# Down projection with seven block products in place of eight in 13 of 44 groups

## The chip, the core and the metric

The kernel runs on one core of a Trainium2 chip, as one launch. The metric is the device time of a launch in microseconds. TensorE (PE) multiplies, VectorE (DVE), ScalarE (ACT) and GpSimd (POOL) work elementwise, and SyncE (SP) issues nearly all DMAs. All matrices are float32. A product of two of them is made of three matmuls in the fp32r format: each operand is split into a high part (a rounding copy) and a low part (operand minus high part), and high x high, high x low and low x high are added up in PSUM.

## The reference

Three layers over 256 tokens of width 2048. The change touches the last step of the third, the feed-forward network, and the final norm behind it:

```python
h = rmsnorm_2(x, ffn_norm[l])
g = causal_dwconv(jnp.einsum('bsd,df->bsf', h, w_gate[l]), conv_w[l], conv_b[l])
u = jnp.einsum('bsd,df->bsf', h, w_up[l])
x = x + jnp.einsum('bsf,fd->bsd', jax.nn.silu(g) * u, w_down[l])   # f = 5632, d = 2048
return rmsnorm_2(x, final_norm)
```

## The kernel before

All weights stream through the core once, as 691 *units* of mostly 128 x 1024 floats (two K tiles of 128 rows by one block of 512 columns, in the down projection). `plan` lists them in order, and every engine walks the same list. SP loads a unit into one of `NS = 4` staging slots (L3027); ACT writes its high part into one of `NR = 3` slots of `s_w` (L1253), after PE has finished the unit three before; DVE subtracts and writes the low part (L1910); PE multiplies (`down`, L706). A staging slot is free once the low part is made.

On ACT and DVE all other work is *side work*: generators in a list (`Side`), each advanced one step by `side.tick()` before each `split()` in `nxt`. So side work stands in program order ahead of a high or low part. `later(n, steps)` holds a generator back by n steps. Both engines' loops stand three units ahead of PE's: what the code puts after `nxt` for a unit comes behind the low part of the third unit after it.

The feed-forward part runs in two halves: 12 blocks of gate and up (L1862, 8 units each), down projection of 24 K tiles, 10 blocks, down projection of 20 K tiles. A gate or up block leaves PSUM by ACT, is turned by 16 DVE transposes of 32x256 (L2001, four a step), then comes the convolution (L2462, L2464, into `CV` from `GG`), silu on ACT, and the product with up (L2477, into one of two `HH`). ACT copies that to the high part of `HID` (L1672) and POOL makes the low part (L2892). The last up block's side work runs while PE is already in the down projection.

The down projection takes the four 512-column blocks n = 0..3 one after the other; tokens are two halves t of 128. Block n's sums lie in PSUM banks `PSS` (n even) or `PST` (n odd), one bank for each t. When a block is done, DVE adds its two banks into `OT` (L2647), which already holds the residual, brought there in the first half by 64 transposes (`flip`, L2634, two a step). In the second half squares of the finished blocks go to ACT (L1679), and POOL multiplies them by the final gain (L3005). The last block's last three units are ordered so that the tail is short (`last_columns`).

Of the kernel before, what the change touches and what calls it, by code (L numbers as in the profile page):

```python
# [23 lines left out]
NTOT = 691  # L24
WINS = (2, 4, 8, 16)
DOWN = (24, 20)
BLOCKS = (range(12), range(12, 22))
PACE = (2,) * 11 + (1,) * 5
# [152 lines left out]
class Plan:  # L181
# [3 lines left out]
    def __init__(self, A):  # L185
        self.A = A
        self.units, self.end, self.bank, self.out, self.half, self.zb = [], {}, {}, {}, {}, []
        self.takes = 0
        self.turned = {}
        self.counts = {"out": 0, "out_act": 0}  # L190
        self.between = Side()

    def unit(self, ap, n, shift=0):
        self.units.append((ap, n, shift))
# [72 lines left out]
    def down(self, hv):  # L267
        for n in range(4):
            for u in range(DOWN[hv] // 2):
                self.unit(self.A["wd"][2 * DOWN[0] * hv + DOWN[hv] // 2 * n + u], 1024, SHIFT)  # L270
                self.step()
            self.end["wd", hv, n] = len(self.units)
# [90 lines left out]
class Memory:  # L363


    def __init__(self, nc, ctx):
# [122 lines left out]
        self.HID = alloc(ff, "hid", [128, 2, DOWN[0], T], F32R)  # L489
        self.EV = alloc(ff, "ev", [128, 4, 2, 128])  # L490
# [3 lines left out]
        self.HH = [alloc(ff, f"hh{i}", [128, T]) for i in range(2)]  # L494
# [7 lines left out]
        self.FW = alloc(ff, "fw", [128, 2])  # L502
        ff.close()
# [25 lines left out]
    def staged(self, c, n):  # L529
        s = self.ST[:, c % NS, 0:n]  # L530
        return s.rearrange("p (k c) -> p k c", k=KT) if n == KT * 36 else s

# [4 lines left out]
    def product(self, bank):  # L537

        if bank[0] == "g":
            return self.PSG[bank[1]]  # L540
        return (self.PSS if bank[0] == "s" else self.PST)[:, bank[1], :]

# [24 lines left out]
def tensor_program(e, S, P, M):  # L567
# [138 lines left out]
    def down(hv):  # L706
# [36 lines left out]
        for n in range(4):  # L743
            for t in range(2):
                vacant(("st"[n % 2], t))
                held["st"[n % 2], t] = ("added", 2 * (4 * hv + n) + t + 1)
            apart = nk // 2 - (3 if hv and n == 3 else 0)
            for u in range(apart):
                w.wait_ge("wl", done[0] + 1)
                products(n, u, done[0] % NR, [(kk, t) for kk in range(2) for t in range(2)]).then_inc(S["units"], 1)  # L750
                unit()
            c = done[0]
            for u in range(apart, nk // 2):
                w.wait_ge("wl", c + u - apart + 1)
                products(n, u, (c + u - apart) % NR, [(0, 0), (1, 0)])
            if apart < nk // 2:
                last_columns(c)
# [482 lines left out]
def scalar_program(e, S, P, M):  # L1240
    w, side, done = Waits(e, S), Side(), [0]

    def split():

        c = done[0]
        if c >= NTOT:
            return
        done[0] += 1
        _, n, shift = P.units[c]
# [3 lines left out]
        e.activation(M.weights(c, 0, n, shift), M.staged(c, n), ACT.Copy).then_inc(S["wh"], 1)  # L1253
# [79 lines left out]
    def token_norm(n, rc, ticks):  # L1333
# [4 lines left out]
        for t in range(2):  # L1338
            w.wait_ge(f"l_tm{i}", 16)
# [324 lines left out]
    def up_block(m):  # L1664
# [3 lines left out]
        for c in range(4):  # L1668
# [3 lines left out]
            e.activation(M.HID[:, 0, j - DOWN[0] * hv, :], M.HH[j % 2][:, :], ACT.Copy).then_inc(S["hidh"], 1)  # L1672
            yield

    def square_out(n, t):
        w.wait_ge("added", 2 * (4 + n) + t + 1)
        if n:
            w.wait_ge("sqx", 2 * n + t - 1)
        e.activation(M.JK[t][:, :], M.OT[:, t, block(n)], ACT.Square, accum_out=M.SS[:, t, n:n + 1]).then_inc(S["sqx"], 1)  # L1679

# [35 lines left out]
    for half, name in enumerate(("st_a", "st0")):  # L1716
        ws = slice(512 * half, 512 * half + 512)
        e.dma_start(M.ST[:, 0, ws], P.units[0][0][:, ws]).then_inc(S[name], 16)
# [142 lines left out]
    for hv in range(2):  # L1861
# [8 lines left out]
        for n in range(4):  # L1870
            nxt(DOWN[hv] // 2)
            if hv and n == 0:
                tables()
            if hv and n < 3:
                side.start(squares(n))
# [23 lines left out]
def vector_program(e, S, P, M):  # L1899
    w, side, done, chained = Waits(e, S), Side(), [0], [0]  # L1900

    def split():

        c = done[0]
        if c >= NTOT:
            return
        done[0] += 1
        _, n, shift = P.units[c]
# [1311 lines left out]
```

## Time and profile before

| | us |
|---|---|
| median of three runs | 1994.98 (1994.73 to 1996.5) |
| the profiled execution: span | 1993.4 |
| PE busy | 1983.1 (99%) |
| DVE busy | 1544.2 (77%) |
| ACT busy | 1067.4 (54%) |
| POOL busy | 404.5 (20%) |

The profile gives its own execution by the span from first to last instruction, and no device time beside it. Down projections run from 1528.1 to 1658.6 us and from 1876.4 to 1985.6 us. A timeline row has start, duration, engine, line, operation, out<-in, partitions x elements and the count it merges; in brackets stands how long the engine idled before it and what ended that. A matmul's duration (0.39 us) reaches into the next, since they are pipelined: what counts is the distance between starts. "PEld" is the load of the stationary operand.

### The profile page before, as it was taken

What the parts mean: (1) busy time and instruction counts of PE and PEld (TensorE: products, weight loads), DVE (VectorE), ACT (ScalarE), POOL (GpSimd) and SP (SyncE); (2) the same over time, 40 slices, a digit from 0 to 9 for tenths busy, and PEclk for the clock granted to TensorE, in tenths of its full rate; (3) what the DMA queues carried; (4) which work ended last, traced back from release to release, by engine and by line L of the source; (5) the groups of instructions that cost most, each with busy time, mean ns of one, the idle gap of its engine ahead of it and who ended that gap; (6) DMA issues with size and microseconds to landing.
All of it is one profiled execution on the core that took longest, in us unless ns stands there. A gap on an engine that the chain in (4) does not pass through costs nothing.

```text
span 1993.4 us, 26947 instructions
## 1 busy us (share of the span) xinstructions
PE 1983.1 (99%) x10228; PEld 1689.0 (85%) x10228; DVE 1544.2 (77%) x2292; ACT 1067.4 (54%) x1625; POOL 404.5 (20%) x381
## 2 busy tenths in 40 slices
PE   9999999999999999999999999999999999999998
PEld 8888888888888888888788888888888888888887
DVE  6876778788798666867777678689899776889954
ACT  7744544467534554654555555455555434555544
POOL 0015543300000444430222235200000000000121
PEclk9999999999999999999999999999999999999999
DMA  9664666567655334565444445655555655555564
GB/s 359 213 198 150 192 185 198 190 210 244 219 172 170 126 117 134 185 218 185 166 162 155 148 155 188 208 190 197 194 190 190 203 196 185 196 191 191 191 205 153
DMA packets 103506, 374.80 MB, mean 188 GB/s; under 512 B 11696, under 2 KB 13136, under 8 KB 102864
## 3 DMA queue, kind: packets, MB, share of 16 engines
q1 hardware_dynamic: 103088, 372.54, 56.3%
q8 instruction: 81, 1.33, 0.3%
q10 hardware_dynamic: 288, 0.52, 0.1%
q14 instruction: 49, 0.40, 0.1%
HBM read 370.92 MB, written 2.10 MB: 187 GB/s over the span
## 4 chain that ended last, share of the span: by engine, by line
PE 98%; DVE 1%; DMA 0%; ACT 0%; issue 0%; ACTq 0%; SPq 0%
PE psg L601 25%; PE psg L602 13%; PE psg L686 9%; PE psg L688 9%; PE psg L687 9%; PE pss L686 4%; PE pss L688 4%; PE pss L687 4%; PE pss L717 2%; PE pss L716 2%; PE pss L718 2%; PE pst L718 2%; PE pst L716 2%; PE pst L717 2%; PE pst L873 1%; PE psg L662 1%
## 5 line engine op out<-in xcount | busy, mean ns | idle before, releaser
L1253 ACT ACTIVATE s_w<-s_stage 128x1024 fp32r<-128x1024 f32 x689 | 724.0, 1053 | 648.6 <-PE psg L602 288.2
L1910 DVE TENSOR_TENSOR s_w<-s_stage,s_w 128x1024 fp32r<-128x1024 f32 x689 | 855.9, 1244 | 269.0 <-ACT s_w L1253 264.7
L601 PE MATMUL psg<-s_rh,s_w 128*128 128x512 f32 x1216 | 427.4, 393 | 0.3 <-DVE s_w L1910 0.3
L601 PE MATMUL psg<-s_ry,s_w 128*128 128x512 f32 x1024 | 361.6, 394 | 0.0
L602 PE MATMUL psg<-s_rh,s_w 128*128 128x256 f32 x1216 | 342.7, 282 | 0.0
L602 PE MATMUL psg<-s_ry,s_w 128*128 128x256 f32 x1024 | 288.4, 282 | 0.0
L601 PEld LDWEIGHTS psg<-s_rh,s_w 128*128 128x128 f32 x1216 | 228.3, 188 | 48.8 <-issue 1.0
L686 PE MATMUL psg<-s_w,s_ry 128*128 128x512 f32 x672 | 263.9, 393 | 0.0
L688 PE MATMUL psg<-s_w,s_ry 128*128 128x512 f32 x672 | 261.7, 389 | 0.0
L687 PE MATMUL psg<-s_w,s_ry 128*128 128x512 f32 x672 | 261.6, 389 | 0.0
L602 PEld LDWEIGHTS psg<-s_rh,s_w 128*128 128x128 f32 x1216 | 229.8, 189 | 0.7
L601 PEld LDWEIGHTS psg<-s_ry,s_w 128*128 128x128 f32 x1024 | 192.3, 188 | 42.1 <-issue 2.7
L602 PEld LDWEIGHTS psg<-s_ry,s_w 128*128 128x128 f32 x1024 | 193.5, 189 | 0.1
L2892 POOL TENSOR_TENSOR s_hid<-s_hh,s_hid 128x256 fp32r<-128x256 f32 x44 | 49.9, 1134 | 581.7 <-ACT s_hid L1672 581.7
L686 PEld LDWEIGHTS psg<-s_w,s_ry 128*128 128x128 f32 x672 | 126.1, 188 | 27.7 <-issue 1.8
L688 PEld LDWEIGHTS psg<-s_w,s_ry 128*128 128x128 f32 x672 | 126.1, 188 | 26.7
L687 PEld LDWEIGHTS psg<-s_w,s_ry 128*128 128x128 f32 x672 | 126.2, 188 | 25.5
L686 PE MATMUL pss<-s_w,s_ry 128*128 128x512 f32 x352 | 137.1, 390 | 0.0
L688 PE MATMUL pss<-s_w,s_ry 128*128 128x512 f32 x352 | 137.1, 389 | 0.0
L687 PE MATMUL pss<-s_w,s_ry 128*128 128x512 f32 x352 | 137.0, 389 | 0.0
L2760 POOL TENSOR_SCALAR s_bsc<-s_bsc,s_stat 128x256 f32<-128x256 f32 (+1 forms) x56 | 46.0, 839 | 187.4 <-DVE s_stat L2355 176.1
L2001 DVE STREAM_TRANSPOSE s_gg<-s_ev 32x256 f32<-32x256 f32 x176 | 76.7, 436 | 2.9
(445 smaller groups left out, 2897.2 us busy)
## 6 DMA issues: line engine op xcount, KB each, us to landing
s_stage<-in_wo SPq DMA_DIRECT2D x96, 512.0 KB, 3.6
s_stage<-in_wg SPq DMA_DIRECT2D x88, 512.0 KB, 3.2
s_stage<-in_wu SPq DMA_DIRECT2D x88, 512.0 KB, 3.3
s_stage<-in_wd SPq DMA_DIRECT2D x88, 512.0 KB, 3.2
s_stage<-in_ain SPq DMA_DIRECT2D x64, 512.0 KB, 3.6
s_stage<-in_wkv SPq DMA_DIRECT2D x32, 512.0 KB, 4.0
s_stage<-in_bq SPq DMA_DIRECT2D x24, 512.0 KB, 3.3
s_stage<-in_bzq SPq DMA_DIRECT2D x24, 512.0 KB, 3.2
```

The lines of the kernel that those rows point to most:

```text
L601: e.matmul(o, M.WH[:, r, ws], xx, start=begin, stop=False)
L602: m = e.matmul(o[:, T:2 * T], M.WL[:, r, ws], xh, start=False, stop=end)
L686: e.matmul(o[:, :], xh[:, ts], M.WH[:, r, ws], start=(k == 0), stop=False)
L687: e.matmul(o[:, :], xh[:, ts], M.WL[:, r, ws], start=False, stop=False)
L688: m = e.matmul(o[:, :], xl[:, ts], M.WH[:, r, ws], start=False, stop=(k == 15))
L716: e.matmul(o, xh[:, ts], M.WH[:, r, ws], start=(k == 0), stop=False)
L717: e.matmul(o, xh[:, ts], M.WL[:, r, ws], start=False, stop=False)
L718: m = e.matmul(o, xl[:, ts], M.WH[:, r, ws], start=False, stop=(k == nk - 1))
L1253: e.activation(M.weights(c, 0, n, shift), M.staged(c, n), ACT.Copy).then_inc(S["wh"], 1)
L1910: e.tensor_tensor(M.weights(c, 1, n, shift), M.staged(c, n), M.weights(c, 0, n, shift), ALU.subtract).then_inc(S["wl"], 1)
L2001: x = e.transpose(dst[32 * r:32 * r + 32, :, :].rearrange("p c (t q i) -> p q t c i", t=2, q=4)[:, q, :, :, :], ev[32 * q:32 * q + 32, r, ...
L2892: e.tensor_tensor(M.HID[:, 1, i, :], M.HH[j % 2][:, :], M.HID[:, 0, i, :].bitcast(F32), ALU.subtract).then_inc(S["hidl"], 1)
```

## The change

The order is now by pairs of blocks (q = 0: n = 0, 1; q = 1: n = 2, 3). For each p (two K tiles) either two plain units, n0 and n1, or, for the p in `SEVEN`, one *group* of four units: X (2 token halves x 2 K tiles) times W (2 K tiles x 2 blocks) by Strassen's scheme in the form with seven products of 128x128 by 128x512. The last p of a pair (the last three in the very last) is done for n0 and then for n1.

- Four sums of X blocks: POOL, from `HH` (now four, two of them `YT`), into `JK`; a high part by ACT and a low part by POOL into `SP` (7 sets, since both pairs of a half use the same).
- Four sums of W blocks: POOL, 128x512 each, two into `TB` (the gate buffer `GG`), two in place in the staging slots. Both slots are given back after the group's last low part.
- Four units with 2, 2, 2 and 1 products; the last is 512 wide. P1, P5, P6, P7 gather in `PSO[0]`, `PSO[1]`, `PSG[0]`, `PSG[1]` over the groups of a pair; the other three go straight into the banks of the blocks.
- After a pair's last group ACT copies P6 out (`sixth`) and DVE folds the four banks into `OT` in eight steps (`fold`), side work.

```diff
-NTOT = 691
+NLOAD = 691
+SEVEN = (((1, 4, 7, 10), (1, 4, 7, 10)), ((1, 4, 7), (1, 4)))
+LASTK = 3
@@ Plan
+    def seven(self, hv, q, p, a, b):
+        c, l = len(self.units), len(self.loads)
+        self.loads += [(a, 1024), (b, 1024)]
+        t = 4 * len(self.sevens)
+        self.sevens[hv, q, p] = (t, c, l, SEVEN[hv][0].index(p) + hv * len(SEVEN[0][0]))
+        self.units += [("raw", l, 1024, SHIFT, 0), ("sum", l, 1024, SHIFT, t + 2), ("raw", l + 1, 1024, SHIFT, t + 3), ("half", l, 512, SHIFT, t + 4)]
+        self.left += [c + 4, c + 4]
+        self.sums_end[hv, q] = c + 4
     def down(self, hv):
+        kp = DOWN[hv] // 2
+        for q in range(2):
...
+            both = kp - (LASTK if hv and q else 1)
+            for p in range(both):
+                if p in SEVEN[hv][q]:
+                    self.seven(hv, q, p, w[0][p], w[1][p])
+                else:
+                    for i in range(2):
+                        self.unit(w[i][p], 1024, SHIFT)
...
@@ tensor_program
+        def three_products(o, ah, al, r, ws, first, last):
+            e.matmul(o, ah, M.WH[:, r, ws], start=first, stop=False)
+            e.matmul(o, ah, M.WL[:, r, ws], start=False, stop=False)
+            return e.matmul(o, al, M.WH[:, r, ws], start=False, stop=last)
+        def seven(q, p):
...
+            if first:
+                vacant(("o", 0))
+            r = done[0] % NR
+            w.wait_ge("wl", done[0] + 1)
+            three_products(M.PSO[0][:, :], h0[:, t0], l0[:, t0], r, w0, first, last)
+            three_products(down_bank(M, 2 * q, 0), h1[:, t0], l1[:, t0], r, w1, False, False).then_inc(S["units"], 1)
+            unit()
+            w.wait_ge("sp_lo", HEADS + idx + 1)
+            if first:
+                vacant(("o", 1), ("g", 1))
...
+            if last:
+                held["o", 0] = ("fold", 8 * g + 2)
+                held["g", 0] = ("p6", g + 1)
+                held["o", 1] = ("fold", 8 * g + 4)
+                held["g", 1] = ("fold", 8 * g + 5)
@@ scalar_program
-        w.wait_ge(f"st{c % NS}", 16 * (c // NS + 1))
+        _, l, n, shift, tee = P.units[c]
+        w.wait_ge(f"st{l % NS}", 16 * (l // NS + 1))
+        if tee:
+            w.wait_ge("tee", tee)
         if c >= NR:
             w.wait_ge("units", c - NR + 1)
@@ vector_program
+    def fold(hv, q):
...
+        w.wait_ge("units", P.sums_end[hv, q])
+        into(0, n0, p1)
+        yield
+        w.wait_ge("p6", 2 * hv + q + 1)
+        e.tensor_tensor(u2, p1, u2, ALU.add).then_inc(S["fold"], 1)
...
+        into(0, n1, p5)
+        yield
+        into(1, n1, p5)
+        yield
...
+        e.tensor_tensor(u3, p7, u2, ALU.add).then_inc(S["fold"], 1)
...
-        for n in range(4):
+        for q in range(2):
             if hv == 0:
-                side.start(flip(n) if n else later(4, flip(n)))
-            nxt(DOWN[hv] // 2)
+                side.start(later(8 if q else 4, flips(q)))
+            ends = hv and q
+            after = LASTK if ends else 1
+            units = P.count[hv, q]
+            side.start(later(P.sums_end[hv, q] - P.end["wd", hv, 2 * q + 1] + units, fold(hv, q)))
+            nxt(units - after)
+            for t in range(2):
+                add_down(hv, 2 * q, t)
+            nxt(after)
...
+                for t in range(2):
+                    add_down(hv, 2 * q + 1, t)
@@ pool_program
+    def weight_sums(hv, q, p):
+        t, c, l, _ = P.sevens[hv, q, p]
+        a, b = M.ST[:, l % NS, :], M.ST[:, (l + 1) % NS, :]
+        tb = M.TB
...
+        w.wait_ge("ff_v", 2 * (DOWN[0] + DOWN[1] * hv))
...
+        e.tensor_tensor(tb[:, 0:512], b[:, 0:512], a[:, 0:512], ALU.subtract).then_inc(S["tee"], 1)
+        e.tensor_tensor(tb[:, 512:1024], b[:, 512:1024], b[:, 0:512], ALU.subtract).then_inc(S["tee"], 1)
+        w.wait_ge("tee", t + 2)
+        e.tensor_tensor(b[:, 0:512], tb[:, 512:1024], a[:, 0:512], ALU.add).then_inc(S["tee"], 1)
+        w.wait_ge("tee", t + 3)
+        w.wait_ge("wl", c + 1)
+        e.tensor_tensor(a[:, 512:1024], a[:, 512:1024], b[:, 0:512], ALU.subtract).then_inc(S["tee"], 1)
@@ sync_program
-            w.wait_ge("wl", c - NS + 1)
+            w.wait_ge("wl", P.left[c - NS])
```

## Rows read from the trace of the kernel before

**Rows 1.** The page: busy time, and the chain that ended last.
```profile
PE 1983.1 (99%) x10228; PEld 1689.0 (85%) x10228; DVE 1544.2 (77%) x2292; ACT 1067.4 (54%) x1625; POOL 404.5 (20%) x381
...
PE 98%; DVE 1%; DMA 0%; ACT 0%; issue 0%; ACTq 0%; SPq 0%
```

**Rows 2.** Windows: length, busy PE, PEld, DVE, ACT, POOL; PEclk, DMA share, GB/s.
```profile
1527.80:1560.60 32.80, 32.80 (x146) 27.15 (x145) 30.21 (x49) 15.69 (x20) 2.98 (x4) 1.00 0.55 188
...
1626.00:1658.60 32.60, 32.60 (x145) 27.01 (x144) 22.79 (x30) 12.77 (x12) 0.00 (x0) 1.00 0.58 195
```

**Rows 3.** Timeline around the end of block 1, first half.
```profile
1593.34 0.39 PE L716 MATMUL pss<-s_w,s_hid 128*128 128x512 f32 x1
...
1593.60 1.06 ACT L1253 ACTIVATE s_w<-s_stage 128x1024 fp32r<-128x1024 f32 x1 [1.66 <-PE pst L718]
...
1594.70 1.23 DVE L1910 TENSOR_TENSOR s_w<-s_stage,s_w 128x1024 fp32r<-128x1024 f32 x1 [1.49 <-ACT s_w L1253]
...
1595.84 1.28 DVE L2647 TENSOR_TENSOR s_ot<-pst,s_ot 128x512 f32<-128x512 f32 x2
...
1596.06 0.39 PE L716 MATMUL pss<-s_w,s_hid 128*128 128x512 f32 x1
```

**Rows 4.** Timeline of the first units of the first half's down projection.
```profile
1528.06 0.39 PE L716 MATMUL pss<-s_w,s_hid 128*128 128x512 f32 x1
...
1530.30 0.48 DVE L2464 SCALAR_TENSOR_TENSOR s_cv<-s_gg,s_vec,s_cv 128x254 f32<-128x254 f32 x1
1530.73 1.23 DVE L1910 TENSOR_TENSOR s_w<-s_stage,s_w 128x1024 fp32r<-128x1024 f32 x1
...
1533.68 1.23 DVE L1910 TENSOR_TENSOR s_w<-s_stage,s_w 128x1024 fp32r<-128x1024 f32 x1
1534.94 1.78 DVE L2001 STREAM_TRANSPOSE s_uu<-s_ev 32x256 f32<-32x256 f32 x4
...
1542.90 1.23 DVE L1910 TENSOR_TENSOR s_w<-s_stage,s_w 128x1024 fp32r<-128x1024 f32 x1
...
1544.18 0.19 PEld L716 LDWEIGHTS pss<-s_w,s_hid 128*128 128x128 f32 x1
1544.38 0.39 PE L716 MATMUL pss<-s_w,s_hid 128*128 128x512 f32 x1
...
1545.27 1.55 DVE L1910 TENSOR_TENSOR s_w<-s_stage,s_w 128x1024 fp32r<-128x1024 f32 x1
```

**Rows 5.** Groups by line: the half-wide high and low parts.
```profile
L1322 ACT ACTIVATE s_w<-s_stage 128x512 fp32r<-128x512 f32 x4 | 2.4, 614 | 0.0
...
L2030 DVE TENSOR_TENSOR s_w<-s_stage,s_w 128x512 fp32r<-128x512 f32 x4 | 2.7, 688 | 0.0
```

**Rows 6.** Timeline: POOL operations beside and apart from DVE's low parts.
```profile
1508.48 1.23 DVE L1910 TENSOR_TENSOR s_w<-s_stage,s_w 128x1024 fp32r<-128x1024 f32 x1 [1.98 <-ACT s_w L1253]
1508.83 1.48 POOL L2892 TENSOR_TENSOR s_hid<-s_hh,s_hid 128x256 fp32r<-128x256 f32 x1 [0.51 <-ACT s_hid L1672]
1544.99 0.75 POOL L2892 TENSOR_TENSOR s_hid<-s_hh,s_hid 128x256 fp32r<-128x256 f32 x1 [34.69 <-ACT s_hid L1672]
1907.70 1.23 DVE L1910 TENSOR_TENSOR s_w<-s_stage,s_w 128x1024 fp32r<-128x1024 f32 x1 [0.30 <-ACT s_w L1253]
1908.35 1.73 POOL L3005 TENSOR_TENSOR s_ot<-s_ot,s_fg 128x512 f32<-128x512 f32 x1 [6.99 <-ACT s_jk L1679]
```

**Rows 7.** Timeline of DVE: two low parts with a flip step between.
```profile
1557.99 1.23 DVE L1910 TENSOR_TENSOR s_w<-s_stage,s_w 128x1024 fp32r<-128x1024 f32 x1
...
1560.15 1.23 DVE L1910 TENSOR_TENSOR s_w<-s_stage,s_w 128x1024 fp32r<-128x1024 f32 x1
```

**Rows 8.** Groups by line, the down phases: adds from PSUM, and ACT's table load.
```profile
L2647 DVE TENSOR_TENSOR s_ot<-pss,s_ot 128x512 f32<-128x512 f32 x8 | 5.1, 684 | 0.0
...
L1261 ACT ACT_TABLE_LOAD x1 | 1.3, 1283 | 0.0
```

**Rows 9.** DMA issues in 1530 to 1620 us, KB each, median us to landing.
```profile
s_stage<-in_wd SPq DMA_DIRECT2D x33, 512.0 KB, 3.2
```

More of the change, by code:

```diff
@@ new lines, in plain @@
+        def plain(n, u):
+            if u == 0:
+                for t in range(2):
+                    vacant(("st"[n % 2], t))
+                    held["st"[n % 2], t] = ("added", 2 * (4 * hv + n) + t + 1)
+            w.wait_ge("wl", done[0] + 1)
+            products(n, u, done[0] % NR, [(kk, t) for kk in range(2) for t in range(2)]).then_inc(S["units"], 1)
+            unit()
+        kp = nk // 2
+        for q in range(2):
+            ends = hv and q
+            paired = kp - (LASTK if ends else 1)
+            for p in range(paired):
+                if p in SEVEN[hv][q]:
+                    seven(q, p)
+                else:
+                    plain(2 * q, p)
+                    plain(2 * q + 1, p)
+            for u in range(paired, kp):
+                plain(2 * q, u)
+            if not ends:
+                plain(2 * q + 1, kp - 1)
+                continue
+            c = done[0]
+            for u in range(paired, kp):
+                w.wait_ge("wl", c + u - paired + 1)
+                products(3, u, (c + u - paired) % NR, [(0, 0), (1, 0)])
+            last_columns(c)
@@ L1869, in scalar_program @@
             side.start(up_block(m) if m % 2 else gate_block(m))
-        for n in range(4):
-            nxt(DOWN[hv] // 2)
-            if hv and n == 0:
-                tables()
-            if hv and n < 3:
-                side.start(squares(n))
+        for q in range(2):
+            units = P.count[hv, q]
+            side.start(later(P.sums_end[hv, q] - P.end["wd", hv, 2 * q + 1] + units, sixth(hv, q)))
+            if not hv:
+                nxt(units)
+            elif q == 0:
+                nxt(10)
+                tables()
+                nxt(units - 10)
+                side.start(later(7, squares(0)))
+                side.start(later(9, squares(1)))
+            else:
+                nxt(units - LASTK)
+                side.start(squares(2))
+                nxt(LASTK)
     side.drain()
@@ L2638, in flip, with flips, into @@
             yield
+    def flips(q):
+        yield from flip(2 * q)
+        yield from flip(2 * q + 1)
+    made = {(t, n): ("flat", 4 * n + 4) for t in range(2) for n in range(4)}
     def add_down(hv, n, t):
         w.wait_ge(*down_done(P, hv, n, t))
-        if hv:
-            w.wait_ge("added", 2 * n + t + 1)
-        else:
-            w.wait_ge("flat", 4 * n + 4)
+        w.wait_ge(*made[t, n])
         x = M.OT[:, t, block(n)]
         e.tensor_tensor(x, down_bank(M, n, t), x, ALU.add).then_inc(S["added"], 1)
+        made[t, n] = ("added", 2 * (4 * hv + n) + t + 1)
+    def fold(hv, q):
+        n0, n1 = 2 * q, 2 * q + 1
+        f = [8 * (2 * hv + q)]
+        def into(t, n, src):
+            w.wait_ge(*made[t, n])
+            x = M.OT[:, t, block(n)]
+            e.tensor_tensor(x, src, x, ALU.add).then_inc(S["fold"], 1)
+            f[0] += 1
+            made[t, n] = ("fold", f[0])
+        p1, p5, p7 = M.PSO[0][:, :], M.PSO[1][:, :], M.PSG[1][:, :]
+        u2, u3 = M.FB2[:, 0, :], M.FB2[:, 1, :]
+        w.wait_ge("units", P.sums_end[hv, q])
+        into(0, n0, p1)
+        yield
+        w.wait_ge("p6", 2 * hv + q + 1)
+        e.tensor_tensor(u2, p1, u2, ALU.add).then_inc(S["fold"], 1)
+        f[0] += 1
+        two = f[0]
+        yield
+        into(0, n1, p5)
+        yield
+        into(1, n1, p5)
+        yield
+        w.wait_ge("fold", two)
+        e.tensor_tensor(u3, p7, u2, ALU.add).then_inc(S["fold"], 1)
+        f[0] += 1
+        three = f[0]
+        yield
+        into(0, n1, u2)
+        yield
+        w.wait_ge("fold", three)
+        into(1, n0, u3)
+        yield
+        into(1, n1, u3)
     def add_last(h):
@@ L3075, in sync_program @@
     e.dma_start(M.FG[:, :], A["fg"]).then_inc(S["l_con2"], 16)
-    while issued[0] < NTOT:
+    while issued[0] < NLOAD:
         weights()
```

208 lines of the change are left out of this document (150 added, 58 removed).

## The prediction

> **What bounds the kernel now.** The page's busy rows and the chain of waits come first: TensorE (PE) is busy 99% of the span and the chain runs through it for 98% [rows 1]. So a matmul taken away is worth its time, provided that nothing else becomes late. The windows over the down projection say the same of the changed stretch: 32.80 us of PE in 32.80 us at granted clock 1.00 (the 2.4 GHz level), while VectorE (DVE) is busy 30.21 us of the first window but only 22.79 us of the last [rows 2]. That leaves the timeline, to see how near the other engines are behind.
>
> Around 1593 us two units' first matmuls start at 1593.34 and 1596.06: 2.72 us for 12 matmuls, 0.2267 us each [rows 3]. Call S(k) the start of unit k. When the unit before 1593.34 has ended, its ring slot is free, ScalarE (ACT) starts the next high part 0.26 us after S (1593.60, 1.06 us) and DVE the low part at 1594.70, which ends at 1595.93 [rows 3]. With three slots this is W(k+3) = S(k+1) + 2.59. Where PE did wait for DVE (low part ended 1542.90 + 1.23 = 1544.13), the weight load began at 1544.18 and the matmul at 1544.38 [rows 4]: S(k) is at least W(k) + 0.25. So a slot needs 2.84 us from release to reuse; plain units give it two units, 5.44 us. The slack is 2.60 us, and DVE spends it: at the start of a down phase it turns a block, four transposes and a low part in 3.07 us (1533.68 to the next one's transposes and back, 1.78 + 1.23 + gaps), against 2.72 us of PE, and at unit 6 nothing is left [rows 4].
>
> **What is removed.** A group computes 7 products of 3 matmuls in place of 8: 13 x 3 x 0.2267 = 8.84 us [rows 3]. The stationary and moving shapes stay. That is 0.44% of the time, and the whole possible gain.
>
> **What the ring does to a group.** The group is now four units of 6, 6, 6 and 3 matmuls: 1.36, 1.36, 1.36, 0.68 us, together 4.76 us where two units took 5.44. ACT and DVE have 3.5 low and high parts where they had two. Let c be its first unit and S(c) = 0. Units c and c+1 got their slots in plain time. Unit c+2 takes the slot of c-1, free at 0: ready for PE at 2.84, wanted at 2.72, 0.12 late. Unit c+3 is half wide (0.61 and 0.69 us [rows 5]) and in time. The plain unit c+4 takes the slot of c+1, free at S(c+2); only c+2 and c+3 cover it, 2.04 us of the 2.84: 0.80 late. So each group loses 0.92 us with nothing beside it and saves 0.68: +0.24, or 13 x 0.92 = 12.0 against 8.84.
>
> **What DVE has beside it.** Its side work is queued ahead of a low part, and it runs three units ahead (the pair of adds after a block stands behind the low part of the third unit on [rows 3]).
> - *First group of each half (p = 1, units 2 to 5).* The four quarters of the last up block's transposes stand ahead of low parts 3 to 6. With S(0) = 0 the low part 2 ends at 3.9 (1530.73 + 1.23 - 1528.06 [rows 4]). The GpSimd (POOL) sums use the gate buffer, so they wait for the last conv operation, which ends at 2.7 [rows 4], then for the port until 3.8. A sum of 128x512 I take at 1.15 us: 1.73 measured, of which 0.58 lay under a low part (1907.70 + 1.23 against 1908.35) [rows 6]. Two sums end at 6.0, ACT's copy of the sum at 7.1, low part 3 at 8.4: S(3) = 8.65, wanted 6.80. Then, a turn (1.80) ahead of each: low part 4 at 11.5, 5 at 14.05, 6 at 17.15; S(6) = 17.4 where 2 x 2.72 + 4.76 = 10.2 would do. 7.2 us lost, and the same in the second half, whose operations stand at the same distances.
> - *Flips of the first half*: two transposes and a low part, 2.16 us [rows 7], ahead of the late parts of p = 4 and 7 in both column pairs. After c+2 ready at 2.59: flip and half part 4.15, flip and part c+4 6.3, so S(c+4) is about 6.55 where 4.76 would do: 1.8 us for three of them. At p = 4 of the first pair DVE has not caught up after the turns and mults (1542.90 to 1545.27 us for the next unit [rows 4] is the pace), and POOL's third and fourth sums hold its port: 3.5 by the same steps. p = 10 has no flips: 0.9, twice.
> - *Change of column pair.* Before, a block's banks were free for a whole block, and the adds (ended 1.19 us after the low part [rows 3]) hid. Now both blocks of a pair end in the last two units and the next pair reuses both bank pairs at once. The first block's adds stand behind the low part of the unit after next: done S + 3.78, PE may go at 4.03, wanted 2.72; the second's the same from there: 2.6 us, in each half. Into the next half's first block it costs 0.7.
> - *Folds.* Eight DVE operations of about 0.68 us (the PSUM add's mean is 684 ns [rows 8]), one ahead of each low part. In the first half p = 1 of the second pair needs PSO[1] and PSG[1], freed by the fifth fold, which stands behind low part c+2 (2.59): S(c+1) = 3.45 where 1.36 would do, and c+4 is 0.8 late: 2.9. In the second half two more plain units lie between, and only late folds cost: 1.3 at p = 1.
> - *ACT* loads a table (1.28 us [rows 8]) inside p = 4 of the second half, 1.05 with the ring; squares in p = 4 of its second pair: 1.35. p = 7: 0.9.
>
> The sum: first half 7.2 + 3.5 + 1.8 + 0.9, change 2.6, 2.9 + 1.8 + 1.8 + 0.9, end 0.7 = 24.1; second half 7.2 + 1.05 + 0.9, change 2.6, 1.3 + 1.35 = 14.4. Together 38.5 lost, 8.8 saved: +29.7 us.
>
> **Edits at nothing.** The sums' waits for their loads: one lands 3.2 us after issue [rows 9] and, issued four units before use, some 5 us ahead; a group's two slots are given back only after its last low part, but the loads they hold up are for units c+6 and c+7, over 6 us later. If that cover went it would be about 1 us a group. Half sums, their copies and low parts (7 sets, four 128x128 and one 128x512 on POOL, one copy on ACT) lie under the gate and up blocks; each could delay a DVE low part by its port time, 0 to 3 us in all, taken as 0. The tail's work on block 2 moves to three units before the end, 8 us ahead of its need: 0 to 0.5, taken as 0. Semaphore and bank renames: nothing.
>
> **Where rule and rows are weighed.** POOL's subtraction of 128x256 took 0.75 us with the port to itself and 1.48 us when it began 0.35 us into a low part, and a low part begun during one took 1.55 instead of 1.23 [rows 6]. So I read the sums as 1.15 us plus what DVE's two-input operations hold, and not as a flat 1.73. The Trainium skill's SBUF — State Buffer, section "Who interferes with whom", says this: a VectorE instruction with two SBUF inputs and a GpSimd instruction that reads SBUF exclude each other for the whole instruction, and one with at most one SBUF input doesn't contend. By it the four sums of a group and its 3.5 low parts cannot overlap at all, which speaks against moving this work to GpSimd. By a flat 1.73 the first groups would start 1.2 us later each, +32.
>
> **Rivals.**
> 1. *The covers hold.* Spare time exists: DVE idles 10 us of 32.6 in the last window [rows 2]. If slots came free earlier than I read, only the matmuls count: 1995.0 - 8.8 = 1986. Against it: two of four fill intervals in a group are shorter than the chain of rows 3, whatever the average is.
> 2. *The ring alone costs.* Side work falls into DVE's waits and the turns hide: 12.0 - 8.8 = +3.1, 1998. For it: DVE is busy 22.79 of 32.60 us once the turns are over, and could catch up [rows 2]. Against: in the first four units of the phase DVE has no wait at all [rows 4], and the bank changes are waits in program order. With the bank changes (5.9) and half of the turns it is 2011.
> 3. *The port.* Each of POOL's 52 sums holds up a low part: in the eight groups with side work, two of 1.15 us each, of which I let half count, 8 x 2.3 x 0.5 = +9 more: 2034. For it: 1.55 us and the zero slack at unit 6 [rows 4]. Against: from c+1's low part to c+2's DVE waits 1.5 us, in which the fourth sum fits.
> 4. *The clock.* PE is now idle for over a third of some 12 us at a time. If the granted clock fell to its 1.2 GHz level there, matmuls would take twice as long: 21 x 0.2267 = 4.8 us in each of the three worst groups, +14: 2039. The rows show 1.00 throughout, but before there was no such gap.
>
> **How the numbers follow.** The sum against the profiled execution is 1993.4 + 29.7 = 2023.1 us of span; the median of the three runs stands 1.6 us above that span, so 2024.5. Chances: the forecast 0.62 (2012 to 2036), rival 2 0.19 (a quarter of it within 0.2%), rival 1 0.07, rivals 3 and 4 together 0.12. About 0.2%, 4 us, is what can be told from no change. Hence faster 0.07, within 0.2% 0.05, slower 0.88. The range cuts rival 1, the light half of rival 2 and the top of 3 and 4: 2001 to 2040.
>
> **What would show it.** 39 matmuls fewer in the down phases, and PE idle before pss/pst/pso/psg units, released by DVE's low parts (`s_w<-s_stage,s_w`), in sum 35 to 40 us. Each step: a wait of 0.8 us before the unit behind every group, even where DVE has no side work; 7 us within the first 18 us of each phase, with the sums' end ahead of the copy of unit 3; twice two waits of 1.3 us on the adds at the change of pair; one of 2 us on a fold. Outside the down phases nothing should move. The prediction is wrong if the unit behind a group starts without a wait, which breaks the ring argument and with it the sign; it is off in size if the first groups' waits are short.

## The result, and the profile after

The changed kernel takes 2032.9 us (median of 5 runs, 2030.9 to 2034.3) against 1995.5 us (1994.7 to 1996.5): a ratio of 1.0188, 95% interval 1.0177 to 1.0199. The profiled execution has a span of 2031.0 us, 37.6 us more than before.

The page: busy time, and the chain that ended last [rows 1].

```profile
PE 1990.3 (98%) x10189; PEld 1682.8 (83%) x10189; DVE 1601.4 (79%) x2350; ACT 1095.0 (54%) x1662; POOL 525.7 (26%) x468
...
PE 88%; DVE 6%; DMA 2%; POOL 2%; ACT 1%; issue 1%; ACTq 0%; SPq 0%; POOLq 0%
```

39 matmuls are gone, and the chain leaves PE for 12% of the span, where it was 2%. PE's busy time didn't fall with them but rose by 7.2 us: the last matmul before a wait counts with its whole 0.39 us, where otherwise the next one starts after 0.23 us, and a matmul at the lower clock shows 0.63 us. Windows over the whole program (length, busy PE, PEld, DVE, ACT, POOL, PEclk, DMA share, GB/s) say where [rows 2]:

```profile
0.00:1528.00 1528.00, 1525.81 (x8196) 1311.67 (x8197) 1192.83 (x1785) 843.63 (x1348) 376.29 (x364) 1.00 0.57 188
1528.00:1682.00 154.00, 134.97 (x553) 103.12 (x551) 124.52 (x165) 70.19 (x76) 65.28 (x41) 0.98 0.48 164
1682.00:1896.00 214.00, 214.00 (x944) 177.18 (x945) 187.16 (x283) 115.12 (x150) 30.63 (x31) 1.00 0.59 192
1896.00:2031.00 135.00, 115.53 (x501) 90.86 (x499) 96.88 (x119) 66.10 (x90) 53.52 (x32) 0.96 0.46 161
```

Nearly all of the loss lies in the two down phases. The first, from its first matmul to the next part's, took 130.56 us and takes 154.31 (+23.75); the second, to the end of the last matmul, 109.3 and 122.2 (+13.0). The feed-forward blocks between them took 217.8 and 217.9. After the last matmul come 1.3 us more.

The first group, up to the plain unit behind it [rows 4]. Columns: start, duration in us, engine, line, tiles, idle time before and what ended it.

```profile
1530.51 2.16 POOL L3114 TENSOR_TENSOR s_gg<-s_stage 128x512 f32<-128x512 f32 x1 [20.65 <-DVE s_cv L2601]
1531.43 1.77 DVE L2138 STREAM_TRANSPOSE s_uu<-s_ev 32x256 f32<-32x256 f32 x4
1532.62 1.29 POOL L3115 TENSOR_TENSOR s_gg<-s_stage 128x512 f32<-128x512 f32 x1
1533.95 1.06 ACT L1365 ACTIVATE s_w<-s_gg 128x1024 fp32r<-128x1024 f32 x1 [3.16 <-POOL s_gg L3115]
...
1535.04 1.32 DVE L2047 TENSOR_TENSOR s_w<-s_gg,s_w 128x1024 fp32r<-128x1024 f32 x1 [1.83 <-ACT s_w L1365]
1535.35 2.13 POOL L3120 TENSOR_TENSOR s_stage<-s_stage 128x512 f32<-128x512 f32 x1
...
1536.39 1.78 DVE L2138 STREAM_TRANSPOSE s_uu<-s_ev 32x256 f32<-32x256 f32 x4
1536.50 0.51 PE L788 MATMUL pso<-s_w,s_sp 128*128 128x512 f32 x1 [1.92 <-DVE s_w L2047]
...
1539.48 0.80 PE L788 MATMUL psg<-s_w,s_sp 128*128 128x512 f32 x1 [0.34 <-DVE s_w L2047]
...
1542.02 0.50 PE L788 MATMUL pss<-s_w,s_hid 128*128 128x512 f32 x1 [0.56 <-DVE s_w L2047]
...
1545.10 0.50 PE L760 MATMUL pss<-s_w,s_hid 128*128 128x512 f32 x1 [2.11 <-DVE s_w L2047]
```

It went as worked out: S(0) = 1527.62, S(3) = 1536.50 is 8.88 later (8.65 forecast), S(6) = 1545.10 is 17.48 later (17.4 forecast). Two sums, the copy of the sum, then a turn ahead of each low part.

The last group of the first pair, which has nothing beside it on DVE [rows 3]:

```profile
1589.27 1.30 POOL L3114 TENSOR_TENSOR s_gg<-s_stage 128x512 f32<-128x512 f32 x1 [7.20 <-issue]
...
1590.52 2.27 POOL L3115 TENSOR_TENSOR s_gg<-s_stage 128x512 f32<-128x512 f32 x1
1592.83 1.06 ACT L1365 ACTIVATE s_w<-s_gg 128x1024 fp32r<-128x1024 f32 x1 [2.70 <-POOL s_gg L3115]
...
1593.92 1.32 DVE L2047 TENSOR_TENSOR s_w<-s_gg,s_w 128x1024 fp32r<-128x1024 f32 x1 [2.28 <-ACT s_w L1365]
...
1594.52 1.06 ACT L1365 ACTIVATE s_w<-s_stage 128x1024 fp32r<-128x1024 f32 x1 [0.63 <-PE pst L762]
```

Its wait isn't where I put it. The forecast was 0.12 us before the third unit and 0.80 behind the group; measured are 0.57 and 0.00. No wait behind a group is what I had named as the sign that the ring argument is wrong. It shows in three of the groups, this one and those at p = 10 of the second pair and p = 7 of the second half. The first sum starts 4.97 us before the group (at 1594.24), and ACT and DVE idle for the sums and not for PE. What ACT waited for in the first down phase (total us, times, longest) says the same, and so do the loads (KB each, median us to landing):

```profile
ACT s_w L1365 <- POOL s_gg L3115: 18.1, 7, 3.2
ACT s_w L1365 <- PE pst L762: 14.0, 12, 1.9
ACT s_w L1365 <- DMA s_stage<-in_wd: 12.9, 6, 3.4
```

```profile
s_stage<-in_wd SPq DMA_DIRECT2D x42, 512.0 KB, 4.3
```

The first sum starts when the group's second block has landed. A block lands 4.3 us after issue (3.2 before [rows 9]), and SP issues a load when its staging slot is free; a group holds two of the four such slots to the end of its last low part. So there were two theories to part: the ring of three split slots (mine), and the ring of four staging slots.

### The profile page after: what moved, and what is told of

The parts are those of the page before. It is cut to its first block, busy times and chain, and to the rows that moved or that the text cites. A ratio compares the mean times of both kernels' runs of the same rounds, so it can differ in the third digit from the quotient of the medians.

```text
span 2031.0 us, 27124 instructions
## 1 busy us (share of the span) xinstructions
PE 1990.3 (98%) x10189; PEld 1682.8 (83%) x10189; DVE 1601.4 (79%) x2350; ACT 1095.0 (54%) x1662; POOL 525.7 (26%) x468
## 4 chain that ended last, share of the span: by engine, by line
PE 88%; DVE 6%; DMA 2%; POOL 2%; ACT 1%; issue 1%; ACTq 0%; SPq 0%; POOLq 0%
PE psg L645 25%; PE psg L646 13%; PE psg L730 9%; PE psg L732 9%; PE psg L731 9%; PE pss L730 4%; PE pss L732 4%; PE pss L731 4%; DVE s_w L2047 3%; DMA s_stage<-in_wd 1%; DVE s_ot L2774 1%; ACT s_w L1365 1%; POOL s_gg L3115 1%; PE psg L706 1%; PE pst L983 1%
## 5 line engine op out<-in xcount | busy, mean ns | idle before, releaser
L1365 ACT ACTIVATE s_w<-s_stage 128x1024 fp32r<-128x1024 f32 (+1 forms) x702 | 732.2, 1045 | 619.3 <-PE psg L646 288.4
L2047 DVE TENSOR_TENSOR s_w<-s_stage,s_w 128x1024 fp32r<-128x1024 f32 (+1 forms) x702 | 876.6, 1251 | 229.0 <-ACT s_w L1365 223.7
L3079 POOL TENSOR_TENSOR s_hid<-s_hh,s_hid 128x256 fp32r<-128x256 f32 x22 | 27.0, 1230 | 341.4 <-ACT s_hid L1784 341.4
```

Of the source, the lines that this page charges most:

```text
L1365: e.activation(M.weights(c, 0, n, shift), M.staged(P.units[c]), ACT.Copy).then_inc(S["wh"], 1)
L2047: e.tensor_tensor(M.weights(c, 1, n, shift), M.staged(P.units[c]), M.weights(c, 0, n, shift), ALU.subtract).then_inc(S["wl"], 1)
L3079: e.tensor_tensor(M.HID[:, 1, i, :], M.HH[j % 4][:, :], M.HID[:, 0, i, :].bitcast(F32), ALU.subtract).then_inc(S["hidl"], 1)
```

## The experiments

All times are medians; the kernel before, measured again beside each variant, took 1995.1 to 1995.6 us. A single group's loss is read from the trace: from its first matmul to that of the unit behind it, less 21 x 0.2267 us.

**The order of pairs alone.** No groups, the pairs' order kept:

```
-SEVEN = (((1, 4, 7, 10), (1, 4, 7, 10)), ((1, 4, 7), (1, 4)))
+SEVEN = (((), ()), ((), ()))
```

> The changed kernel's order of the down units (the two blocks of a pair by turns, both ending in the last two units) without any group: all 44 pairs of units have eight products, and the sums, folds and the copy of product six are left out. Computes the reference. It prices the change of column pair alone. Theory (bank reuse, my term of 2.6 us in each half and 0.7 us into the next half): 1995.5 + 5.9 = 2001.4 us, with two waits of about 1.3 us on DVE's adds before the second pair in each half. Rival (adds hide as before, and what the changed kernel lost there came from the folds beside it): 1995.5, within 1 us.

Measured: 1998.8 us, ratio 1.0018 (1.0009 to 1.0027), so +3.7 us, with one wait at each change of pair and one into the next half:

```profile
1594.34 0.47 PE L760 MATMUL pss<-s_w,s_hid 128*128 128x512 f32 x1 [1.00 <-DVE s_ot L2788]
...
1660.23 0.51 PE L730 MATMUL pss<-s_w,s_ry 128*128 128x512 f32 x1 [0.36 <-DVE s_ot L2788]
```

The mechanism holds, but I had its size more than twice too high: PE loses 1.16 us at each change, not 2.6. Once the first block has waited, the second block's adds are done in time.

**The first group of each half left out.**

```
-SEVEN = (((1, 4, 7, 10), (1, 4, 7, 10)), ((1, 4, 7), (1, 4)))
+SEVEN = (((4, 7, 10), (1, 4, 7, 10)), ((4, 7), (1, 4)))
```

> The changed kernel without the first group (p = 1 of the first column pair) of each half: 11 groups in place of 13. Computes the reference. Each of the two groups lost 7.28 us of PE by the trace and saved 0.68. Theory (the loss comes where a group meets the turned transposes, and plain units have enough slack for them): 2032.9 - 13.2 = 2019.7 us, and the group at p = 4 of the first half loses under 3.7 us. Rival (the backlog of DVE only moves into the next group, p = 4): that group loses 6 us or more, and the time stays above 2025.

Measured: 2024.1 us, 8.8 us less than the changed kernel and not 13.2. The group at p = 4 now loses 4.77 us in the first half (3.70 with the first group) and 3.74 in the second (2.34). In the first half another 0.78 us of wait stand right before it, and the change of pair behind it loses 3.0 us (2.07). So part of the backlog does move on, as the rival said, though less than it said.

**Four split slots.** The fourth lies in a tensor of its own; the final gain is loaded later, over half of x:

```
-            w.wait_ge("units", c - NR + 1)
+            w.wait_ge("units", c - (4 if c >= FROM[0] + 3 else 3) + 1)
```

> The changed kernel with a fourth split weight slot from the feed-forward part of the third layer on (the room is found by loading the final gain later, over a buffer that is free by then). Computes the reference. Theory (three slots are the limit: 2.84 us from release to reuse): a unit has 2.7 us more of cover, the waits of 0.5 to 0.9 us before the third unit of a group and of 1.5 us behind it go, the first groups lose 2.7 us less each: 13 x 1 + 2 x 2.7 less, 2032.9 - 18 = 2015 us. Rival A (the sums, which wait for their loads in four staging slots, set the third unit, not the ring): waits before the third unit stay, -4 to -6 us, 2027 to 2029. Rival B (DVE has no time at all beside its work): within 2 us of 2032.9.

Measured: 2032.5 us, no change. The first theory, three slots as the only limit, fell. But ACT now waited for loads instead of PE, longest 5.0 us; and the feed-forward part had become slower (below).

**The sums of weights left out** (the second to fourth unit of a group split raw blocks, so the products have other values).

```
-        return self.TB
+        return self.ST[:, l % NS, 0:n]
```

> The changed kernel with the sums of weight blocks left out: the second, third and fourth unit of each group split the raw weight blocks, so the products are of other values than the reference's; all loads, splits, matmuls, half sums and folds stay. It prices POOL's 52 sums. Theory as in the prediction (sums cost where they hold up low parts and the copy of the third unit, the ring and DVE's side work the rest): first groups 2.5 us less each, the eleven others 0.3 to 1 us less: 2032.9 - 5 - 7 = 2021 us, and the waits behind groups with flips and folds stay at about 1.5 us. Rival (POOL's sums are the whole cause): all waits in groups go, -36, 1997. Rival (they cost nothing): 2032.9.

Measured: 2022.5 us, 10.4 less. Waits in the groups fall from 36.75 to 25.4 us, and in three groups with nothing beside them they become 0.53 to 0.55 us *behind* the group, which is the place that my ring argument gave (0.80 forecast):

```profile
1597.61 0.50 PE L760 MATMUL pss<-s_w,s_hid 128*128 128x512 f32 x1 [0.38 <-DVE s_w L2047]
```

The 10.4 us understate what the sums cost: in this trace 24 matmuls behind the two first groups came 0.43 us apart and not 0.23, some 5 us, where the changed kernel has eight such outside its groups.

**Six staging slots; then six and four.** The staging ring gets two more slots; for both, the half sums' buffers and the conv buffers share room with tiles that are free by then.

```
-        if c >= NS:
-            w.wait_ge("wl", P.left[c - NS])
+        if st_old(c) is None:
+            w.wait_ge("units", P.end["wo2", KT - 1])
+        elif st_old(c) >= 0:
+            w.wait_ge("wl", P.left[st_old(c)])
```

> The changed kernel with six staging slots for arriving weight blocks in place of four, from the third layer's feed-forward part on; still three split weight slots. Computes the reference. The run with four split slots changed nothing, and its trace shows why it may be so: a group gives its two staging slots back only after its last low part, four loads are then issued at once, ScalarE waits 3.4 to 5.0 us for them, and POOL's first sum starts at the landing, 5 us before the group. Theory (the staging ring, not the ring of split weights, was the limit there): the sums start 2.7 us or more earlier, the wait of 0.4 to 0.9 us before the third unit of 11 groups goes; but with three split slots the plain unit behind the group then waits the 0.8 us of the prediction where nothing else holds it: 11 x 0.7 less, at most 3 x 0.8 more, and 1 us less in each first group: 2032.9 - 8 = 2025 us (2022 to 2029). Rival (loads wait on the DMA engines, not on slots): landings stay at 5 us before the group, within 2 us of 2032.9.

> The changed kernel with both: six staging slots and four split weight slots, from the third layer's feed-forward part on (two pairs of small buffers and the final gain share room with buffers that are free by then). Computes the reference. Theory (two rings in series, each of which hides the other): waits of groups without flips or folds go below 0.2 us, those with flips fall from 1.5 us behind the group to under 0.5 us, the first groups lose 5 us in place of 7.3, the change of column pair keeps its 2 us: 36.75 us of waits fall to about 14, 2032.9 - 22 = 2011 us (2006 to 2017). Rival A (DVE has no time beside flips and turns; slots only move the wait): 2025 to 2029, the same as with six staging slots alone. Rival B (the staging alone decides): no difference from six staging slots alone, within 2 us.

Measured: 2033.0 us with six staging slots alone, 2019.7 with both. Each alone leaves the time as it was, both give 13 us: two rings in series, and each hides the other. With six and three, waits for loads are gone from ACT's list, the last group of the first pair starts its first sum 5.7 us ahead and its second ends in time; it loses 0.00 before the third unit and 0.53 behind:

```profile
1590.37 1.32 POOL L3143 TENSOR_TENSOR s_gg<-s_stage,s_st 128x512 f32<-128x512 f32 x1 [8.06 <-issue]
1591.64 1.29 POOL L3144 TENSOR_TENSOR s_gg<-s_stage 128x512 f32<-128x512 f32 x1
...
1601.47 0.50 PE L789 MATMUL pss<-s_w,s_hid 128*128 128x512 f32 x1 [0.37 <-DVE s_w L2076]
```

The slots are only a part of that. The second block of this group is now issued 12.9 us ahead of it and not 9.9, but with more loads in flight it takes 7.0 us to land and not 4.8, so 0.8 us are left (the rival's point). Another 1.0 us comes from what stands beside the second sum: no low part here, so that it takes 1.29 us where it took 2.27.

With both, 8 of 13 groups lose at most 0.07 us. The first groups still lose 7.2, and those with flips 2.3 to 3.6.

**The fourth slot moved.** With a fourth slot the feed-forward blocks, which no group touches, had slowed. Windows of the same 100 us, in the run with both rings and then with the slot moved:

```profile
1300.00:1400.00 100.00, 100.00 (x438) 81.89 (x437) 88.02 (x135) 56.19 (x78) 13.11 (x13) 1.00 0.58 192
```

```profile
1300.00:1400.00 100.00, 100.00 (x443) 82.76 (x442) 88.75 (x137) 57.35 (x79) 13.16 (x13) 1.00 0.56 195
```

```
+        self.PADW = alloc(ff, "padw", [128, (wb - nc.sbuf_base - 1) % 256 // 4 + 1])
         self.W3 = alloc(ff, "w3", [128, 2, UWP], F32R)
```

> As the run with six staging and four split slots, with the fourth split slot moved by 96 bytes, so that it lies at the same place modulo 256 bytes as the other three. Computes the reference. Reason: in the runs with a fourth slot the feed-forward blocks, which no group touches, became slower: 438 matmuls in 100 us where the changed kernel has 443, and every fourth unit of 12 matmuls took 2.79 to 2.81 us in place of 2.72. Theory (the place of that one slot slows its weight loads): back to 2.72 us, 443 matmuls; some 530 us of the feed-forward part at 1.1% is 5.8 us, with the down units 7: 2019.7 - 7 = 2013 us, and then the run with four split slots alone, at the same fault, would also have gained about 7 us, not 0. Rival (a second tensor for the slot, or four slots as such, cost that time, by conflicts of DVE's and ACT's writes with TensorE's reads): 2019.7.

Measured: 2013.9 us, 5.8 less, and the units' length is that of the kernel before again. (The pad is 224 bytes, not the 96 I wrote: the fourth slot lay 32 bytes further, modulo 256, than the other three; this undoes it. It also moves what is allocated behind the slot.) So the four-slot run's "no change" had hidden a gain. Its feed-forward blocks had lost 2.7 us ahead of the first down phase and 2.3 ahead of the second, and another 2.2 us of its traced execution lie earlier, where it doesn't differ from the changed kernel; the lengths of the down phases alone tell:

```
                        first down   second down   both, against the changed kernel
changed kernel            154.3        122.0
four split slots          151.1        119.9         -5.2
six staging slots         154.1        121.3         -0.9
both                      143.9        115.5        -16.8
both, fourth moved        143.5        114.5        -18.2
```

(Us from the first down matmul to the next part's, or to the start of the last matmul.) The two alone give 6.1 us added up, both at once 16.8 at the same place of the fourth slot: the conclusion stands.

**Ten groups, where DVE has room.** Same slots; the flips get a list of units.

```
+SEVEN = (((7, 10), (1, 4, 7, 10)), ((4, 7), (1, 4)))
+FLIPS = ((*range(4, 14), 12, 13, *range(18, 22)), (*range(8, 18), 16, 17, *range(22, 26)))
```

> The same slots, with ten groups where DVE has room: none at p = 1 and p = 4 of the first column pair of the first half, none at p = 1 of the first pair of the second half; and the transposes of the residual (flips) are kept out of the groups at p = 7 and 10 of the first pair and p = 7 and 10 of the second, two units in each pair taking two steps to make up. Computes the reference. Theory (a group takes 4.4 us of DVE's low parts in 4.76 us, so it pays where nothing else stands beside it and both rings cover it; measured 0.06 us there): 10 x 0.68 saved, 0.1 us lost in each, the change of pair 0.8, the tail 1.25, 1 us unaccounted: 1995.1 - 6.8 + 1 + 3 = 1992.3 us (1990 to 1995), faster than before. Rival (DVE at 95% of the first half cannot take seven-product groups wherever the flips stand; the waits come back before plain units): 1997 or more.

Measured: 1996.1 us, ratio 1.0004 (0.9995 to 1.0013): the same as before. In the down phases 6.8 us are saved, 6.0 us lost in waits and some 1.5 in matmuls that came a little slower. The two largest waits had my own doubled steps ahead of a group's second and third low part:

```profile
1565.41 1.77 DVE L2825 STREAM_TRANSPOSE s_ot<-s_x 32x256 f32<-32x256 f32 x4
...
1567.21 1.50 DVE L2098 TENSOR_TENSOR s_w<-s_gg,s_w 128x1024 fp32r<-128x1024 f32 x1
...
1568.74 1.78 DVE L2825 STREAM_TRANSPOSE s_ot<-s_x 32x256 f32<-32x256 f32 x4
...
1571.83 0.50 PE L839 MATMUL psg<-s_w,s_sp 128*128 128x512 f32 x1 [1.35 <-DVE s_w L2098]
```

**Three variants of it.** First the flips placed by DVE's program, not PE's; then an eleventh group; then the first of them with the old slots.

```
+FLIPS = ((*range(4, 12), *range(15, 20), *range(23, 26)), (*range(8, 16), *range(19, 24), *range(27, 30)))
```

> The ten groups and the slots of the run before, with DVE's transposes of the residual placed three units earlier against the groups: that run still lost 1.90 and 1.91 us before the third unit of two groups, where DVE's trace shows two doubled steps (1.77 us each) ahead of the low parts of the group's second and third unit; DVE's program runs three units ahead of TensorE, and I had placed them as if by TensorE's units. No doubled step now. Computes the reference. Theory (DVE's program order there is the cause): both waits go, 1996.1 - 3.8 = 1992.3 us, faster than before by 0.15%. Rival (the sums or the slots hold the third unit): 1996 us.

> As the run with ten groups and placed transposes, with an eleventh group, p = 4 of the first pair of the first half, and the transposes kept out of it but for one doubled step. Computes the reference. Theory (DVE is still behind from the turned transposes of the last up block there; the group adds 1.94 us of DVE work for 0.68 of TensorE): it loses 1 to 2.5 us, so 0.3 to 1.8 us slower than with ten. Rival (only the transposes beside it made it lose): 0.7 us faster than with ten.

> The same ten groups and the same places of the transposes, with the changed kernel's slots (four staging, three split). Computes the reference. It prices the slots once no side work stands beside a group. Theory (without them each group loses 0.5 to 0.9 us, before its third unit, or 0.8 behind it, and the bank waits grow): 10 x 0.8 + 2 = 10 us over the run with the slots, 2002 us. Rival (with the side work away three slots do): within 2 us of the run with the slots.

Measured: 1997.8 us (ratio 1.0012, 1.0003 to 1.0021), 2003.0 and 2018.1. In the first the waits inside the ten groups do fall, from 4.8 us to 1.4, so the cause was right; but the time doesn't follow. The late flips now stand with the folds ahead of the adds at the change of pair, where PE loses 3.1 us (1.2 in the run before), and 1.1 us go into the next half (none before):

```profile
1590.10 0.89 DVE L2825 STREAM_TRANSPOSE s_ot<-s_x 32x256 f32<-32x256 f32 x2
1591.02 2.12 DVE L2098 TENSOR_TENSOR s_w<-s_stage,s_w 128x1024 fp32r<-128x1024 f32 x1
1593.07 0.68 DVE L2855 TENSOR_TENSOR s_ot<-pso,s_ot 128x512 f32<-128x512 f32 x1
1593.67 1.70 DVE L2098 TENSOR_TENSOR s_w<-s_st,s_w 128x1024 fp32r<-128x1024 f32 x1
...
1595.29 1.28 DVE L2845 TENSOR_TENSOR s_ot<-pss,s_ot 128x512 f32<-128x512 f32 x2
...
1596.67 0.77 PE L811 MATMUL pss<-s_w,s_hid 128*128 128x512 f32 x1 [2.97 <-DVE s_ot L2845]
```

The run with twelve groups below, whose flips end earlier, has neither wait. The eleventh group cost 5.2 us and not 0.3 to 1.8: it lost 2.9 itself and 2.0 at the next group. The old slots cost 20 us where I forecast 10: 20.4 us in the groups against 1.4.

**Twelve groups.**

```
+SEVEN = (((7, 10), (1, 4, 7, 10)), ((4, 6, 8), (2, 4, 6)))
+FLIPS = ((*range(4, 12), 8, 9, *range(15, 20), 16), (*range(8, 16), 11, 12, *range(19, 24), 20))
```

> Six staging and four split slots, as in the runs with ten groups. Transposes of the residual kept out of the low parts of groups, as in the run before, but ended by unit 23 of each pair (four and five doubled steps between groups), so that they no longer stand ahead of the folds and the adds of a pair's end, where that run lost 3.13 and 1.06 us; and in the second half, where DVE has no transposes, groups at p = 4, 6, 8 and 2, 4, 6 in place of 4, 7 and 1, 4: twelve groups. Computes the reference. Theory (each group now saves its 0.68 us; 1.5 us lost in groups, 1.2 at the change of pair, 0.6 at the table load, 1 us of slower matmuls, 0.8 later start): 1995.6 - 8.2 + 5.1 = 1992.5 us. Rival A (three groups with only one plain pair between are too dense for the sums and loads; they lose 1 us or more each): 1996 to 1998. Rival B (the doubled steps bring back the waits of 1.6 us): 1995 to 1996.

Measured: 2005.5 us, worse than the theory and both rivals. 6.1 us go in one group, p = 6 of the second half. Its first sum stands in POOL's program behind the last hidden tiles and their half sums, which keep POOL busy from 1898.66 to 1909.14 us, and so starts 1.3 us before the group (1910.42) where the one of the last group above stood 5.7 us ahead. The tail is 2.5 us longer besides:

```profile
1906.51 1.43 POOL L3134 TENSOR_TENSOR s_hid<-s_yt,s_hid 128x256 fp32r<-128x256 f32 x2
1907.90 1.29 POOL L3156 TENSOR_TENSOR s_sp<-s_et,s_sp 128x512 fp32r<-128x512 f32 x1
1909.14 2.27 POOL L3169 TENSOR_TENSOR s_gg<-s_stage,s_st 128x512 f32<-128x512 f32 x1
1911.38 1.27 POOL L3170 TENSOR_TENSOR s_gg<-s_stage 128x512 f32<-128x512 f32 x1
...
1915.22 0.47 PE L839 MATMUL pso<-s_w,s_sp 128*128 128x512 f32 x1 [3.18 <-DVE s_w L2098]
```

Its first half, with the same six groups and the flips ended by unit 23, took 131.2 us (133.8 with the late flips, 130.6 in the kernel before).

No version beat the kernel before. The second half alone did: with four groups it took 107.8 us in three of the runs, against 109.0. Groups in the second half only would so give about 1.2 us, an estimate from these traces, less than the 1.8 us either way of the interval with ten groups; it wasn't run.

## Why the prediction was right, and where it wasn't

The slowdown was forecast for the right reason, PE's waits for what ACT, DVE and POOL must do per group, and the time fell 8 us above the forecast. Part of the nearness is luck, as the ring below shows. (1993.4 + 29.7 + 1.6 is 2024.7, not 2024.5.) The sum, 38.5 us lost and 8.8 saved, against the trace (us of PE):

```
step                                    forecast    measured
first group of each half                7.2, 7.2    7.28, 7.28
first half, first pair, p = 4, 7, 10    3.5, 1.8, 0.9    3.70, 2.76, 0.71
first half, second pair, p = 1, 4, 7, 10   2.9, 1.8, 1.8, 0.9   2.63, 2.18, 2.59, 1.14
second half, p = 4, 7; then 1, 4        1.05, 0.9; 1.3, 1.35   2.34, 1.04; 0.84, 2.26
change of pair, first and second half   2.6, 2.6    2.07, 1.79
into the next half                      0.7         1.34
tail                                    0           1.3
start of the first down phase           0           -0.4
rest of the difference                  0           3.7
```

Lost are 46.5 us, of which 36.75 in the groups (32.6 forecast); less 8.8, the span grows by 37.6 where I had 29.7. Of the rest, 1.6 us are the lower clock behind the change of pair (below); 2.1 us stay untraced.

- **The first groups** were right in mechanism, and to 0.1 us in size: turns, sums and low parts in one queue.
- **The fold** was right: at p = 1 of the second pair the second unit waited 1.94 us for the fold that frees PSG[1]:

```profile
1616.95 0.68 DVE L2819 TENSOR_TENSOR s_uu<-psg,s_uu 128x512 f32<-128x512 f32 x1
...
1617.73 0.47 PE L788 MATMUL pso<-s_w,s_sp 128*128 128x512 f32 x1 [1.78 <-DVE s_uu L2819]
```

- **The ring** was the step that failed. I wrote "0.80 late" behind each group and took the sums' waits for their loads at nothing ("If that cover went it would be about 1 us a group"). That cover was gone: the second block of a group lands 5 us before it, two sums (1.3 and 2.3 us) and a copy follow, and the third unit is 0.4 to 0.7 us late in 11 of the 13 groups. The wait before the third unit then gives the unit behind the group its cover back, since its slot is released earlier than it starts. So two faults gave about the right sum, which is luck. A fourth split slot would by my text have recovered 12 us; it recovered 5.2, two more staging slots 0.9, both 16.8.
- **The change of pair** measured 2.07 and 1.79 with folds beside it, but 1.16 by itself: 2.6 was two waits where one covers the other.
- **The tail** I took at 0. It is 1.3 us: DVE's adds and last folds of the second half's second pair end late. It is 0 in six of the seven runs with four split slots, and 2.5 us with twelve groups.
- **The port** (rival 3): a sum takes 1.27 to 1.30 us alone (I took 1.15), and 2.13 to 2.29 beside a low part; low parts took up to 2.18 us behind a sum. That is what the Trainium skill states, SBUF — State Buffer, section "Who interferes with whom", and the other half of its rule shows too: transposes, with one SBUF input, took 1.78 us beside a sum (1536.39 above) as without one [rows 4]. Of the 100 full-width low parts of both down phases 36 took over 1.28 us, 12.1 us more in all than at 1.23 (POOL's other work included); how much of that reached PE is not told apart, so it proves nothing that 2032.9 lies nearer to this rival's 2034 than to my 2024.5.
- **The clock** (rival 4) did fall, but in three stretches of about 3 us, and it cost 1.6 us and not 14. Two stretches lie inside the first groups, where DVE sets the time. With the moved slot that group's clock stayed at 1.00, and it lost 7.27 us all the same; the windows are 12.1 us in both runs, the changed kernel first:

```profile
1533.00:1545.10 12.10, 7.17 (x22) 4.38 (x21) 9.96 (x18) 4.87 (x5) 4.33 (x3) 0.86 0.17 59
```

```profile
1533.50:1545.60 12.10, 5.86 (x23) 3.56 (x21) 9.96 (x18) 4.65 (x5) 4.36 (x3) 1.00 0.16 60
```

  The second stretch cost: PE lost 2.07 us at 1607.26, and was soon after granted its 1.2 GHz level, eight matmuls 0.43 us apart:

```profile
1606.00:1609.00 3.00, 1.74 (x7) 1.47 (x8) 3.00 (x4) 0.50 (x1) 2.68 (x3) 0.91 0.81 285
1609.00:1612.00 3.00, 3.00 (x9) 2.31 (x8) 2.64 (x4) 0.23 (x1) 2.92 (x2) 0.52 0.02 8
1612.00:1615.00 3.00, 3.00 (x15) 2.46 (x14) 1.82 (x2) 1.12 (x2) 0.36 (x1) 1.00 0.00 0
```

- **DVE's time** is the likely reason why nothing beat the kernel before. A group asks 4.4 us of DVE (3.5 low parts) where two plain units ask 2.5, and gives PE 0.68 us; the folds come on top. Windows over the first down phase, the kernel before and then the one with ten groups:

```profile
1528.10:1658.60 130.50, 130.50 (x577) 108.07 (x576) 99.99 (x140) 54.01 (x56) 2.98 (x4) 1.00 0.57 195
```

```profile
1528.80:1661.20 132.40, 128.58 (x559) 104.11 (x559) 122.98 (x164) 65.95 (x72) 51.61 (x33) 1.00 0.53 190
```

  DVE was busy 100.0 us and is busy 123.0, where 558 matmuls need 126.5: hardly any spare time is left, and each wait in DVE's order reaches PE. In the second half, which has no flips, four groups did save 1.2 us. No run took work from DVE alone to prove it.

## What to carry to other kernels

Before cutting work from the engine that bounds a kernel, write down what each of its feeders has per saved step: here 0.68 us of TensorE was bought with 1.9 us of VectorE and the folds, and in the first down phase that took VectorE from 77% busy to 93% even with ten groups. When a pipeline passes two rings in series, enlarge both before judging either, and look at phases the edit should not touch, since a new buffer's place alone cost 5.8 us here. Place side work by the program order of the engine that runs it (VectorE is three units ahead here), and ask of each shift what stands behind it at the next boundary.

## What the hardware showed unexpectedly

- A split weight slot 32 bytes further, modulo 256, than the others made every fourth unit of 12 matmuls take 2.79 to 2.81 us in place of 2.72 in the feed-forward blocks (438 against 443 matmuls in 100 us). By the kernel's allocation that slot's remainder was 160, as is that of the normed x which these matmuls multiply with, where the other slots' is 128. Whether the equal remainders or another conflict does it was not tried.
- A PE wait of some 2 us was followed by a stretch at the lower clock in some cases and not in others of the same length. In the changed kernel's down phases PE was idle six times for 1.78 to 2.12 us at once: after 1.92, 1.91 and 1.92 us the granted clock fell to 0.50 to 0.52 for about 3 us, although PE worked on, and then was 1.00 again; after 2.11, 2.12 and 1.78 us it stayed at 1.00. Without the sums it fell after both waits of 2.12 us. So the length of the one wait doesn't decide it. Before, PE had no wait in the down phases and the clock stayed at 1.00.
